# Sums of squares moved to VectorE, the norm factors broadcast a few chunks earlier, and another order of the summed operands, in a streaming encoder layer

## The reference, cut to what matters

```python
x = x + 0.5 * swiglu(rmsnorm(x, ffn1_norm), ffn1_w_gate, ffn1_w_up, ffn1_w_down)   # D_FF = 2816
h = rmsnorm(x, mix_norm)
z = h @ w_in                      # gated conv, q, k, v, and the indexer's q, k, weights
...                               # rotations, token selection, attention
x = x + jnp.concatenate([conv_out, attn], axis=-1) @ w_out
x = x + 0.5 * swiglu(rmsnorm(x, ffn2_norm), ffn2_w_gate, ffn2_w_up, ffn2_w_down)

def rmsnorm(x, g):
    y = x * rsqrt(mean(x * x) + EPS)
    return y * g
def swiglu(x, w_gate, w_up, w_down):
    return (silu(x @ w_gate) * (x @ w_up)) @ w_down
```

## Time and profile before

| | |
|---|---|
| time, median of 3 runs (lowest to highest) | 1250.52 us (1247.56 to 1251.45) |
| time of the profiled execution | 1250.03 us |
| its span | 1248.2 us |
| TensorE busy | 1205.1 us, 97% |
| VectorE busy | 806.3 us, 65% |
| ScalarE busy | 483.5 us, 39% |
| GpSimd busy | 327.9 us, 26% |
| mean granted TensorE clock | 0.985 |

### The profile page before, as it was taken

The page is one execution under the profiler, slowest core; times in us unless marked ns, Lnnn a source line. Parts: engine busy times, 40 slices in busy tenths (PEclk is TensorE's granted clock), DMA queues, the critical chain, the costliest instruction groups (busy, mean ns, idle before and its releaser), DMA issues.

```text
span 1248.2 us, 20666 instructions
## 1 busy us (share of the span) xinstructions
PE 1205.1 (97%) x7992; PEld 1158.9 (93%) x7992; DVE 806.3 (65%) x1030; ACT 483.5 (39%) x716; POOL 327.9 (26%) x238
## 2 busy tenths in 40 slices
PE   8989999999999999989899899998999999999998
PEld 8989999999999999857899679998999999999998
DVE  4898777876335442377998844769877777733533
ACT  5344444444324333341122453424444444423321
POOL 4235444451000102003663000412545454100000
PEclk9989999999999999999899999999999999999999
DMA  6111212122332233100311021320122222133222
GB/s 243 68 35 68 101 67 101 69 99 67 110 126 69 67 109 120 68 34 35 135 68 35 1 62 43 144 102 34 68 81 88 93 75 101 51 117 119 77 75 101
DMA packets 24069, 103.83 MB, mean 83 GB/s; under 512 B 3536, under 2 KB 4944, under 8 KB 16592
## 3 DMA queue, kind: packets, MB, share of 16 engines
q1 hardware_dynamic: 23136, 99.28, 22.6%
q10 hardware_dynamic: 880, 3.82, 1.0%
HBM read 96.99 MB, written 6.10 MB: 83 GB/s over the span
## 4 chain that ended last, share of the span: by engine, by line
PE 80%; DVE 12%; ACT 3%; issue 2%; POOL 1%; DMA 1%; ACTq 0%; DVEq 0%; POOLq 0%
PE ps L488 12%; PE ps L490 12%; PE ps L492 12%; PE ps L526 11%; PE ps L528 11%; PE ps L527 11%; PE ps L479 2%; PE ps L481 2%; PE ps L480 2%; PE ps L689 2%; DVE wl L1390 1%; PE ps L812 1%; DVE wl L1285 1%; POOL sqacc L1828 1%; DVE xs L1377 1%
## 5 line engine op out<-in xcount | busy, mean ns | idle before, releaser
L932 ACT ACTIVATE wh<-raw 128x1024 fp32r<-128x1024 f32 (+3 forms) x185 | 191.4, 1036 | 390.2 <-PE ps L492 280.1
L526 PE MATMUL ps<-xs,wh 128*128 128x320 f32 x720 | 224.7, 312 | 12.7 <-issue 9.1
L527 PE MATMUL ps<-xs,wh 128*128 128x320 f32 x720 | 224.1, 311 | 0.0
L528 PE MATMUL ps<-xs,wl 128*128 128x320 f32 x720 | 224.0, 311 | 0.0
L1285 DVE TENSOR_TENSOR wl<-raw,wh 128x1024 fp32r<-128x1024 f32 (+2 forms) x65 | 104.4, 1606 | 181.8 <-ACT wh L932 181.8
L488 PE MATMUL ps<-xs,wh 128*128 128x320 f32 x704 | 160.5, 309 | 1.5 <-DVE xs L1459 1.5
L490 PE MATMUL ps<-xs,wh 128*128 128x320 f32 x704 | 160.5, 309 | 0.0
L492 PE MATMUL ps<-xs,wl 128*128 128x320 f32 x704 | 160.3, 309 | 0.0
L1390 DVE TENSOR_TENSOR wl<-raw,wh 128x1024 fp32r<-128x1024 f32 (+1 forms) x108 | 147.3, 1365 | 7.9 <-ACT wh L932 5.9
L526 PEld LDWEIGHTS ps<-xs,wh 128*128 128x128 f32 x720 | 136.3, 189 | 14.5 <-issue 10.0
L488 PE MATMUL ps<-xh,wh 128*128 128x320 f32 x576 | 139.5, 324 | 6.2 <-DVE wl L1285 4.3
(11 more groups left out here) (202 smaller groups left out, 2041.4 us busy)
## 6 DMA issues: line engine op xcount, KB each, us to landing
raw<-gu SPq DMA_DIRECT2D x43, 1024.0 KB, 4.8
raw<-dn SPq DMA_DIRECT2D x44, 512.0 KB, 3.3
raw<-wconv SPq DMA_DIRECT2D x6, 1024.0 KB, 4.8
raw<-wout SPq DMA_DIRECT2D x4, 1024.0 KB, 4.8
raw<-wtok SPq DMA_DIRECT2D x4, 840.0 KB, 4.4
x<-xt SPq DMA_DIRECT2D x8, 320.0 KB, 3.7
x_keep<-x SPq DMA_DIRECT2D x8, 320.0 KB, 2.2
x<-x_keep SPq DMA_DIRECT2D x8, 320.0 KB, 3.8
```

Source lines behind the costliest of these rows:

```text
L526: pe.matmul(out, ah, bh, start=first, stop=False, skip_group_check=True)
L527: pe.matmul(out, ah, bl, start=False, stop=False, skip_group_check=True)
L528: return pe.matmul(out, al, bh, start=False, stop=last, skip_group_check=True)
L932: return nc.scalar.activation(out, in_, ACT.Copy, scale=scale)
```

## The change

VectorE makes the seven additions of squares of each stage in place of GpSimd: three of them in the midst of the low parts of the operands and the rest later, in stage 0; after each low part, in stages 1 and 2. TensorE takes the column sums and the broadcast earlier: in the first FFN ahead of chunk 0 and chunk 4 of unit 1 (before: chunks 4 and 7), in the second after the second and third quarter of unit 0 (before: after the third quarter, and ahead of chunk 4 of unit 1). VectorE and ScalarE make the operands of the set units in another order. No instruction is added or left out.

```diff
@@ tensor, ffn(k)
+                    if k and part == 1:
+                        column_sums(stage)
                     if k and part == 2:
-                        column_sums(stage)
+                        broadcast_rstd(stage)
...
                 for c in range(C):
+                    if k == 0 and c == 0:
+                        column_sums(stage)
                     if k == 0 and c == 4:
-                        column_sums(stage)
-                    if c == (7, 4)[k]:
                         broadcast_rstd(stage)
                     glu_part(1, 0, c)
@@ scalar, ffn(k)
                 plain_tanh(0)
+                operand_out(0, xn_ready, C * (k + 1))
                 act.wait_ge(unit_done, first + 2)
                 split_hi(None, base // 2 + 1, 1, 2048)
                 plain_tanh(1)
-                operand_out(0, xn_ready, C * k + 4)
                 operand_out(1, xn_ready, C * (k + 1))
+                operand_out(2, xt_ready, 4 * k + 2)
+                operand_out(3, xt_ready, 4 * k + 2)
                 act.wait_ge(unit_done, first + 3)
                 set_hi_of(0, 0, 0)
                 set_hi_of(0, 0, 1)
-                operand_out(2, xt_ready, 4 * k + 2)
+                operand_out(4, xt_ready, 4 * (k + 1))
                 plain_tanh(2)
-                operand_out(3, xt_ready, 4 * k + 1)
-                operand_out(4, xt_ready, 4 * k + 4)
-                snapshot(0, 0, 0)
+                operand_out(5, xt_ready, 4 * (k + 1))
                 act.wait_ge(unit_done, first + 4)
                 set_hi_of(0, 0, 3)
+                snapshot(0, 0, 0)
                 set_hi_of(0, 0, 2)
...
@@ vector
+            def add_squares(stage, c):
+                dve.wait_ge(sq_ready, C * stage + c + 1)
+                if c > 1:
+                    dve.wait_ge(sq_added, (C - 1) * stage + c - 1)
+                dve.tensor_tensor(sqacc[:, :], sqacc[:, :], (sq, sq_odd)[c % 2][:, :], ALU.add)\
+                    .then_inc(sq_added, 1)
...
+                    for c in range(1, 4):
+                        add_squares(0, c)
                     split_lo(2, 1, 2048)
+                    for c in range(4, C):
+                        add_squares(0, c)
                 else:
                     for c in range(4, C):
                         operand_lo(2, c)
+                        add_squares(2, c)
...
@@ gpsimd, norm_factors(stage)
-                for c in range(1, C):
-                    add_squares(stage, c)
```

More of the change, by code:

```diff
@@ L1085, in ffn @@
                 set_hi_of(0, 0, 1)
-                operand_out(2, xt_ready, 4 * k + 2)
+                operand_out(4, xt_ready, 4 * (k + 1))
                 plain_tanh(2)
-                operand_out(3, xt_ready, 4 * k + 1)
-                operand_out(4, xt_ready, 4 * k + 4)
-                snapshot(0, 0, 0)
+                operand_out(5, xt_ready, 4 * (k + 1))
                 act.wait_ge(unit_done, first + 4)
                 set_hi_of(0, 0, 3)
+                snapshot(0, 0, 0)
                 set_hi_of(0, 0, 2)
-                operand_out(5, xt_ready, 4 * k + 4)
-                snapshot(0, 0, 1)
                 act.wait_ge(xo_lo, 7 * k + 6)
                 operand_out(6, xt_ready, 4 * k + 3)
+                snapshot(0, 0, 1)
                 snapshot(0, 0, 2)
@@ L1460, in hidden_lo @@
                                       hh[:, s, :].bitcast(F32), ALU.subtract).then_inc(hl_ready, 1)
-                plain_out(0, 0)
-                split_lo(base + 3, 0, 2048)
-                plain_hid(0)
                 if k:
@@ L1468, in ffn @@
                     normalised(c)
+                plain_out(0, 0)
+                split_lo(base + 3, 0, 2048)
+                plain_hid(0)
+                for c in range(4, C):
+                    normalised(c)
+                operand_rest(0)
                 plain_out(1, 1)
@@ L1471, in ffn @@
                 plain_hid(1)
[L1472 to L1475, removed]
                 token_sum(X_SOURCE[3], quadrant(0, 1), quadrant(0, 0))
@@ L1479, in ffn @@
                 token_sum(X_SOURCE[2], quadrant(1, 1), X_SOURCE[3])
+                operand_rest(1)
                 dve.wait_ge(xt_ready, 4 * k + 2)
@@ L1482, in ffn @@
                 token_sum(quadrant(1, 0), quadrant(1, 0), X_SOURCE[2])
+                dve.wait_ge(xt_ready, 4 * k + 3)
+                operand_rest(2)
+                operand_rest(3)
+                token_sum(X_SOURCE[4], quadrant(1, 1), quadrant(0, 1))
                 plain_out(2, 0)
@@ L1485, in ffn @@
                 set_rest(0, 0, 1)
-                dve.wait_ge(xt_ready, 4 * k + 3)
-                operand_rest(2)
-                plain_hid(2)
-                operand_rest(3)
-                token_sum(X_SOURCE[4], quadrant(1, 1), quadrant(0, 1))
                 dve.wait_ge(xt_ready, 4 * (k + 1))
                 operand_rest(4)
+                plain_hid(2)
+                operand_rest(5)
                 plain_out(3, 1)
@@ L1495, in ffn @@
                 set_rest(0, 0, 2)
-                operand_rest(5)
                 operand_rest(6)
@@ L1530, in ffn @@
                             operand_lo(1, c)
+                            if c:
+                                add_squares(1, c)
                 if k == 0:
@@ L1807, in _ @@
                     operand_lo(2, b - (NPROJ + NOUT + 4))
+                    if b > NPROJ + NOUT + 4:
+                        add_squares(2, b - (NPROJ + NOUT + 4))
             ffn(1)
@@ L1822, in root @@
                 return pool.tensor_tensor(out, in_, half_pow[:, 0:in_.shape[1]], ALU.pow)
-            def add_squares(stage, c):
-                pool.wait_ge(sq_ready, C * stage + c + 1)
-                if (C - 1) * stage + c - 1:
-                    pool.wait_ge(sq_added, (C - 1) * stage + c - 1)
-                pool.tensor_tensor(sqacc[:, :], sqacc[:, :], (sq, sq_odd)[c % 2][:, :], ALU.add)\
-                    .then_inc(sq_added, 1)
             def norm_factors(stage):
-                for c in range(1, C):
-                    add_squares(stage, c)
                 pool.wait_ge(var_ready, stage + 1)
```

## The result

The changed kernel takes 1238.95 us (median of 4 runs, 1235.64 to 1239.92), the one before 1249.99 in the runs beside it. The ratio is 0.9909, with a 95% interval of 0.9895 to 0.9924: some 11 us less. Forecast were 1239 us and a gain of 11.7.

What follows compares the result with a forecast made beforehand. VectorE's list from `rbc` to set (0,1)'s last weight low part was taken to bound the set phase's start. Gains 6.3 + 0.9 + 4.5 = 11.7 us off 1250.03 give 1238.3, median 0.5 higher, so 1239; range 1235 to 1245.

Steps and rivals of the forecast that it cites:

- The bound: First FFN: VectorE's list from `rbc` (36.11) to set (0,1)'s last weight low part (99.88) bounds the set phase's start.
- The price of an addition: Additions of squares on VectorE: 0.74 us each, 0.1 more when waiting for the one before; GpSimd takes 1.57 to 2.55.
- The list: VectorE, first FFN from 33.2: 39.4 us of work, 1.4 for operand 0, 6.0 of GpSimd collisions, ending at 80.0.
- First FFN: Product 4 of set unit (0,1) starts at 94.8 instead of 101.15, a gain of 6.3 us.
- Second norm: Down products: without GpSimd's collision the low part is ready at 411.8 instead of 412.7, a gain of 0.9 us.
- Third norm: Second FFN: product 4 of (0,1) at 880.8 instead of 885.27, gaining 4.5 us including a new 1.65 us wait.
- The clock: Slow TensorE stretches after the waits in (0,1), 1.4 and 1.5 us lost, were both kept in the forecast.
- more slow stretches: Rival, chance 0.20: new column-sum waits each bring 1.5 us of slow clock, or collisions cost 1 to 3 us; 1241 to 1244.
- The clock holds: Rival, chance 0.13: both slow TensorE stretches after the waits in (0,1) go, giving 1236 us.
- Slower: Rival, chance 0.05: an addition on VectorE costs what GpSimd needs, 1.97 us each; 1252 us.
- the reordering's alone, hence 1243: If the shared port makes the additions bring nothing, only the new order gains, about 7.9 us, giving 1243.
- Half the gain: Rival, chance 0.09: VectorE's list ends as late, unit 3's weights held back; first FFN gains 1, not 6.3; 1244 to 1248.

Runs made afterwards that it cites:

- experiment 8: The kernel before with one line moved: ScalarE's snapshot 0 of set unit (0,0) ahead of the high part of operand 4; 1249.28 us, ratio 0.9996.
- experiment 2: The kernel before with the additions of squares on VectorE and nothing else; 1244.20 us, ratio 0.9952.
- experiment 1: The changed kernel with the additions of squares back on GpSimd, new places and order kept; 1247.49 us, ratio 0.9984.
- 4, old places: The changed kernel with the column sums and the broadcast where they were before; 1236.24 us, ratio 0.9891.
- experiment 5: The changed kernel with column sums and broadcast later: first FFN unit 1 chunks 2 and 5, second FFN unit 0 chunk 6 and last quarter; 1233.40 us, ratio 0.9876.
- experiment 9: The changed kernel with each of the 21 additions preceded by one of the same size into an unread buffer; 1252.40 us, ratio 1.0029.
- Experiment 3: The kernel before with the new order of the operands on ScalarE and VectorE and nothing else; 1242.09 us, ratio 0.9932.
- 6: The changed kernel with VectorE's plain_hid(3) put behind the first two periods; 1238.15 us, ratio 0.9913.
- 7: The changed kernel with both the later column sums and broadcast and the late plain_hid(3); 1232.36 us, ratio 0.9856.
- 11: The changed kernel with plain_hid(3) behind the first two periods, timed again beside the unaltered changed kernel; 1236.08 us, ratio 0.9907.
- experiment 10: The changed kernel as it is, timed and profiled again; 1237.09 us, ratio 0.9895 to the kernel before.

## Why the prediction was right, and where its terms were off

**The bound.** That VectorE's list from `rbc` to the last weight low part of (0,1), and not the snapshot, bounds the start of the set phase in the first FFN, is shown by experiment 8, and by how the eight traces below agree. The list starts at the first instruction after the norm factors; TensorE's product 4 of (0,1) is where its last low part is waited for.

| kernel | list starts | product 4 of (0,1) | from one to the other |
|---|---|---|---|
| before | 36.11 | 101.15 | 65.04 |
| 2, additions alone | 34.29 | 99.32 | 65.03 |
| 8, snapshot first | 37.78 | 102.85 | 65.07 |
| changed | 35.34 | 96.23 | 60.89 |
| 1, additions back on GpSimd | 39.47 | 100.36 | 60.89 |
| 4, old places | 34.76 | 95.78 | 61.02 |
| 5, later column sums | 32.97 | 93.85 | 60.88 |
| 9, each addition twice | 41.48 | 102.37 | 60.89 |

The start moves by 8.5 us, and the length knows only the order: 65.0 us with the old one, 60.9 to 61.0 with the new. Experiment 3, with the new order, has 62.0, of which 1.05 are one wait for TensorE at a slow clock; 6, 7 and 11 have less work in it. The prediction says that VectorE works "nearly without a pause" in it. In fact it had pauses of 4.3 us before. The order took away one of 0.25 and these two, each a wait for ScalarE's high part of an operand:

```profile
79.49 1.49 DVE L1377 TENSOR_TENSOR xs<-xd,xs 128x1280 fp32r<-128x1280 f32 x1 [1.41 <-ACT xs L932]
...
86.93 1.49 DVE L1377 TENSOR_TENSOR xr<-x,xr 128x1280 fp32r<-128x1280 f32 x1 [1.34 <-ACT xr L932]
```

That is 3.0 of the 4.15 us by which the list is shorter. The other 1.1 is one instruction fewer that is stretched beside GpSimd's weight sums (six before, five after). In the second FFN the list is not what bounds the changed kernel: the same stretch takes 66.3 us there, and 61.0 and 61.1 in experiments 3 and 4, where the list starts 13.7 us after the second quarter of unit 0 and not 9.8. In it VectorE itself waits 2.12 and 3.00 us for TensorE, so there TensorE's own work and its waits count.

**The price of an addition.** 0.74 us, with 0.1 to 0.2 for the wait on the one before: the rows have 0.82 busy and 0.93 from start to start (17.68, 18.61). Right, as are the end of the sums (forecast 26.4, measured 26.9) and the waits for them (1.4 and 1.65, measured 1.35 and 1.53). That the first wait fits is luck in part: TensorE came to the place at 25.7 in this execution and at 24.6 in that of experiment 10, where it waited 2.42 us.

**The list.** The estimate was 46.8 us from its start to the end of the low part that product 4 waits for. It was 46.1 (35.34 to 81.4); for collisions with GpSimd's weight sums 6.0 were put in, and five rows are stretched, by 5.1 in all. The block behind it was put at 12.7 and took 12.7 (83.39 to 96.1). A wait at product 4 of 1.8 was forecast and 1.20 came; in the second FFN none, and none came.

**First FFN: 6.3 forecast, 4.9 measured.** The step that was off is the time of the broadcast, "26.5 + 1.0 + 3.5 = 31.0". It came at 33.33. The column sums were 0.6 us late, at 27.07, and the column sums and four parts behind them took 6.3 us instead of 4.5, since they ran partly at 1.2 GHz: 18 matmuls in 4 us instead of 29. VectorE therefore started at 35.34 instead of 33.2. In experiment 5 the column sums stand at 27.09 and the clock is full behind them; with three parts between, the broadcast comes 3.9 us later. A fourth part of 0.9 would make it 4.7, so the slow clock cost 1.5 us. The forecast gain was to be 2.9 us of earlier start and 3.4 of a shorter list; it was 0.8 and 4.15.

**Second norm: 0.9 forecast, 0.9 measured.** The low part was no longer held up and TensorE waited 0.51 instead of 1.46.

**Third norm: 4.5 forecast, 3.2 measured**, again with a slow stretch (19 matmuls instead of 29, 1.4 us) behind the new wait. By experiments 2 and 3 the order alone brings 4.65 here and the additions alone nothing.

**The clock.** I kept both slow stretches behind the waits of (0,1) and gave new ones behind the column sums to a rival, *more slow stretches*, at 1.5 us each. In both profiled executions of the changed kernel the two new ones came, so that rival's mechanism is what happened, at 1.5 and 1.4 us. Of the two old ones, one went. The old ones I had priced too high, at 1.4 and 1.5 us. From product 4 of (0,1) to the down products it is 310.7 us with a slow stretch (the changed kernel) and 310.2 without (experiments 4 and 5), and in the second FFN from there to the end of the span 362.9 with (before) and 362.5 without (the changed kernel). So each costs 0.5 us: at full clock TensorE waits another 0.79 us at product 6, which the slow stretch hides. *The clock holds* could have brought 1 us and not 2.9. The rule of the Trainium skill that I set against the rows, "TensorE: Matmul & The Clock Gate", section "What's actually happening", by which the short waits would cost no clock, is not what these runs show: the clock fell behind waits of 1.35 and 1.53 us, though not behind 1.84 at 875.64.

**Luck.** The terms that were off cancel in part: -1.4 and -1.3 in the two FFNs against +0.5 at the end, where the old stretch went, and +0.5 in the mixer, which is chance. That makes 10.1 for the profiled execution where 11.7 was forecast, 1239.92 where 1238.3 was. It was also the slowest of the four, so that the median, 1238.95, meets the forecast of 1239 more closely than the terms deserve.

**The rivals.** *Slower* decided "from 1.8 us an addition on"; experiment 9 puts the point lower. With 1.67 us from one addition to the next the kernel was 0.3% slower than before, 3.6 us, and with 0.93 it was 11.7 faster beside it; a straight line between the two, an estimate, crosses at 1.5. The working left out what a long wait costs in clock. The rule of the Trainium skill that speaks against the change, "Perfetto Trace Analysis", section "Optimizing Scalar/DVE Operations", that moving work between GpSimd and VectorE may not help, does not come true in this case: the additions alone bring 6 us by the ratio (experiment 2), and with them back on GpSimd the kernel has 1247.5 against 1237 to 1239 us (experiment 1). VectorE makes an addition in 0.82 us where GpSimd takes 1.57 alone. The working "the reordering's alone, hence 1243" was itself right: experiment 3 has 1242.1. *Half the gain* did not come: unit 3 had its weights in time.

**What the prediction didn't see** is that one part of the change works against it. With the additions on VectorE and the new order, the old places give 1236.2 and the new ones 1237.1 to 1239.0; later places, by two chunks in the first FFN, give 1233.4. The first of these differences is within what the times can tell, and rests on the traces (0.4 and 1.3 us in the two FFNs). I had counted the early places as a gain of the first FFN.

## What to carry to other kernels

When the matmul engine waits inside a stage whose operands another engine makes, read that engine's whole list from the event that starts it: the instruction that the wait names may be only the first of several that are late, and removing it moves the wait. To see whether the list is the bound, measure from its first instruction to the wait in several kernels: if the start moves and the length stays, it is. Then look for the pauses within it. An early reduction on TensorE was worth most in this kernel where its input was just ready; two chunks earlier it cost the wait and then the clock. When work is moved between GpSimd and VectorE, compare the two durations of that very form, and count the instructions that each had held up in the other.

## What was not expected of the hardware

A wait of 1.35 us on TensorE was followed by a stretch at a granted clock of 0.57 over 4 us (18 matmuls instead of 29). Behind a wait of 6.74 us 7 us ran at 0.50 (28 matmuls), and the clock was low already in the last 3 us of the wait (0.58). Whether a given wait costs clock varied. At the first column sums, waits of 1.04, 1.35, 1.41, 1.88 and 2.42 us were followed by a slow stretch (experiments 8, the changed kernel, 11, 3 and 10), and one of 1.59 was not (before), nor one of 0.57 (experiment 5). The same wait of 1.8 us at product 4 of (0,1) was followed by one in six of nine traces in the first FFN, and in three of ten in the second; within one execution of the changed kernel, at 96.23 but not at 875.64.

What such a stretch costs hangs on what comes next. Behind the column sums, with the broadcast waiting for TensorE, it cost all of its 1.5 us. Behind product 4 of (0,1), where TensorE would soon have waited for VectorE anyway, it cost 0.5.
